# Forgetting attention: key blocks aligned with the query tiles, first 16 keys of two heads handled together

## The reference

```python
starts = [0] + list(range(N_META, L, BLOCK_Q))       # 0, 16, 144, 272, 400
ends = starts[1:] + [L]
for q0, q1 in zip(starts, ends):
    tpos = jnp.arange(q0, q1)[:, None]
    spos = jnp.arange(q1)[None, :]
    causal = spos <= tpos
    ...
    s = jnp.einsum('bhqd,bhkd->bhqk', qb[:, :, q0:q1], kb[:, :, :q1]).astype(jnp.float32) * scale
    s = s + c[:, :, q0:q1, None] - c[:, :, None, :q1]
    p = jax.nn.softmax(jnp.where(causal, s, -jnp.inf), axis=-1)
    out_fox.append(jnp.einsum('bhqk,bhkd->bhqd', p.astype(vb.dtype), vb[:, :, :q1]))
```

## Time and profile before

| | us |
|---|---|
| median of 3 runs | 1782.82 |
| lowest and highest of them | 1781.14, 1783.95 |
| the profiled execution's own time | 1780.38 |
| its span, from first to last instruction | 1778.4 |
| attention steps in it (500 to 636) | 136 |
| one pair of heads in the loop | 30.2 |

### The profile page before, as it was taken

How to read it: one execution, slowest core, us unless ns; L and a number is a source line. 1 busy time by engine, 2 the same in 40 slices (tenths; PEclk the granted TensorE clock), 3 DMA queues, 4 the chain that set the end, 5 groups by cost and what they waited for, 6 DMA issues and landing times.

```text
span 1778.4 us, 34436 instructions
## 1 busy us (share of the span) xinstructions
PE 1756.8 (99%) x13692; PEld 1702.2 (96%) x13692; DVE 1403.8 (79%) x2020; ACT 942.1 (53%) x1554; POOL 65.1 (4%) x170
## 2 busy tenths in 40 slices
PE   8999999999999999999999999999999999999998
PEld 8999999999988899999999999999999988899997
DVE  7857998779978857947998789479987688499975
ACT  5534655565567744533655545336555445266555
POOL 0000000002122201000000000000000000000000
PEclk9999999999999999999999999999999999999999
DMA  5242333336564422333333333333333323244332
GB/s 165 75 131 84 109 106 96 99 87 195 175 173 133 119 60 84 95 107 84 109 107 96 100 91 96 108 83 109 106 96 88 91 71 107 71 119 119 96 93 74
DMA packets 335157, 187.07 MB, mean 105 GB/s; under 512 B 18976, under 2 KB 325728, under 8 KB 335008
## 3 DMA queue, kind: packets, MB, share of 16 engines
q1 hardware_dynamic: 331568, 175.63, 35.3%
q0 software_dynamic: 2608, 8.72, 1.3%
q10 hardware_dynamic: 832, 0.62, 0.1%
HBM read 171.51 MB, written 10.82 MB: 103 GB/s over the span
## 4 chain that ended last, share of the span: by engine, by line
PE 82%; DVE 10%; issue 3%; ACT 3%; DMA 1%; SPq 0%; POOL 0%; DVEq 0%; ACTq 0%; POOLq 0%
PE pair L2577 46%; PE pair L2549 17%; PE pair L2518 8%; PE pair L2911 3%; PE pair L2564 1%; PE pair L847 1%; DVE w_lo L1995 1%; PE pair L2753 1%; DVE w_lo L2011 1%; PE pair L2840 1%; DVE w_lo L2006 1%; PE pair L2786 1%; PE pair L831 1%; DVE sums_w L1979 1%; PE pair L788 1%
## 5 line engine op out<-in xcount | busy, mean ns | idle before, releaser
L2577 PE MATMUL pair<-b_hi,w_hi 128*128 128x264 f32 (+1 forms) x1464 | 416.7, 285 | 2.0 <-DVE b_lo L2146 1.6
L2577 PE MATMUL pair<-b_hi,w_lo 128*128 128x264 f32 (+1 forms) x1464 | 414.7, 283 | 0.0
L2577 PE MATMUL pair<-b_lo,w_hi 128*128 128x264 f32 (+1 forms) x1464 | 414.6, 283 | 0.0
L2577 PEld LDWEIGHTS pair<-b_hi,w_hi 128*128 128x128 f32 x1464 | 275.8, 188 | 4.2 <-issue 2.9
L2577 PEld LDWEIGHTS pair<-b_lo,w_hi 128*128 128x128 f32 x1464 | 275.9, 188 | 0.0
L2577 PEld LDWEIGHTS pair<-b_hi,w_lo 128*128 128x128 f32 x1464 | 275.5, 188 | 0.0
L1513 ACT ACTIVATE w_hi<-sums_w 128x1024 fp32r<-128x1024 f32 x188 | 198.6, 1056 | 104.1 <-PE pair L2577 61.0
L1513 ACT ACTIVATE w_hi<-raw_all 128x1024 fp32r<-128x1024 f32 (+1 forms) x188 | 158.9, 845 | 141.7 <-PE pair L2577 100.1
L2577 PE MATMUL pair<-blocks_hi,w_hi 128*128 128x264 f32 (+1 forms) x816 | 231.7, 284 | 0.8 <-ACT parts L1696 0.8
L2577 PE MATMUL pair<-blocks_hi,w_lo 128*128 128x264 f32 (+1 forms) x816 | 231.2, 283 | 0.0
L2577 PE MATMUL pair<-blocks_lo,w_hi 128*128 128x264 f32 (+1 forms) x816 | 231.2, 283 | 0.0
(11 more groups left out here) (344 smaller groups left out, 3809.9 us busy)
## 6 DMA issues: line engine op xcount, KB each, us to landing
raw_all<-in_w_ffn_in SPq DMA_DIRECT2D x173, 512.0 KB, 3.9
raw_all<-in_w_ffn_out SPq DMA_DIRECT2D x64, 512.0 KB, 4.3
raw_all<-in_w_ffn_out SPq DMA_DIRECT2D x32, 384.0 KB, 3.6
raw_all<-in_w_attn_in SPq DMA_DIRECT2D x24, 512.0 KB, 4.4
qk_dram<-qk_hi POOLq DMA_DIRECT2D x16, 264.0 KB, 4.1
qk_dram<-qk_lo POOLq DMA_DIRECT2D x16, 264.0 KB, 2.9
raw_all<-in_w_attn_out SPq DMA_DIRECT2D x8, 512.0 KB, 4.8
head_v<-v_tok SPq DMA_DIRECT2D x16, 160.0 KB, 2.6
```

The source lines that it names most:

```text
L2577: mm = nc.tensor.matmul(dst, w[slot][:, c0 + kk * P:c0 + (kk + 1) * P], rhs(v, kk), start=(fresh and kk == 0 and w is w_hi and v == 0), st ...
```

## The change

**Blocks.** A forgetting tile's own key blocks now start at key 16, so they are aligned with the query tiles: s + 1 blocks of 128 keys, and the first 16 keys apart. The values of kind 1 are laid out alike (`value_tile`): four tiles from key 16 on, and keys 0 to 15 as the fifth.

**The first 16 keys.** The first head's probabilities start at column 0 of `probs[s]`, the second head's at column 16. Since both heads of a pair use the same buffer for the same s, the first head's 16 first-key columns stay at 0 to 15 and the second head's land at 16 to 31. `turn` of the second head transposes these 32 columns (with what stands behind them, 128 in all) in one block. `fox_values` of the second head multiplies 32 partitions: 16 keys of one head and 16 of the other, against a fifth tile of `head_v[1]` whose partitions 0 to 15 hold the first head's values in their 64 columns, and whose partitions 16 to 31 hold the second's.

**The small tile** is turned and multiplied once a pair, at g = 4, with both heads' 16 columns, instead of at g = 0 and g = 4.

**Staging and zeroing.** `stage_v` takes four tiles of kind 1, and for the second head two more small copies. The copies of kind 1 in pair 0 wait for a third zeroing on GpSimd. The memsets of padding columns go, and so do ScalarE's waits on them.

```diff
-        first_probs = sb("first_probs", [P, META], F32, late)
-        first_turned = sb("first_turned", [P, META], F32, late)
+        first_probs = sb("first_probs", [P, 2 * META], F32, late)
+        first_turned = sb("first_turned", [2 * META, META], F32, late)
...
-        def probs_pad(s):
-            return probs[s][:, META + (s + 1) * P:(s + 2) * P]
+        def own_probs(g):
+            at = META * (g // 4)
+            return probs[g % 4][:, at:at + fox_tile(g)[1]]
+        def own_block(g, b):
+            at = META * (g // 4) + META + b * P
+            return probs[g % 4][:, at:at + P]
+        def meta_probs(g):
+            return probs[g % 4][:, 0:P]
...
+        def value_tile(kind, jt):
+            if kind == 0:
+                return key_tile(jt)
+            return (META + jt * P, P) if jt < QT - 1 else (0, META)
...
             def stage_v(hp, e, kinds=(0, 1)):
                 for kind in kinds:
-                    sp.dma_start(head_v[e][:, kind, :, HD * e:HD * (e + 1)],
-                                 v_tok[:, kind, :, bass.ds((2 * hp + e) * HD, HD)]).then_inc(staged_v[e], 16)
+                    tiles = slice(0, QT - kind)
+                    sp.dma_start(head_v[e][:, kind, tiles, HD * e:HD * (e + 1)],
+                                 v_tok[:, kind, tiles, bass.ds((2 * hp + e) * HD, HD)]).then_inc(staged_v[e], 16)
+                if e == 1 and 1 in kinds:
+                    for a in range(2):
+                        sp.dma_start(head_v[1][META * a:META * (a + 1), 1, QT - 1, HD * a:HD * (a + 1)],
+                                     v_tok[0:META, 1, QT - 1, bass.ds((2 * hp + a) * HD, HD)]).then_inc(staged_v[e], 16)
...
+                if kind == 1:
+                    sp.wait_ge(v_zero, 3)
...
                 sc = p_psum(g)
-                for b in range(s + 2):
-                    cols = slice(b * P, (b + 1) * P)
-                    mm = nc.tensor.transpose(sc[:, cols], probs[s][:, cols], ident[:, :])
-                if s == 0:
+                for b in range(s + 1):
+                    mm = nc.tensor.transpose(sc[:, b * P:(b + 1) * P], own_block(g, b), ident[:, :])
+                if e == 1:
+                    mm = nc.tensor.transpose(sc[:, (s + 1) * P:(s + 2) * P], meta_probs(g), ident[:, :])
+                if g == 4:
                     pe.wait_ge(first_p, 2 * hp + e + 1)
-                    mm = nc.tensor.transpose(sc[0:META, FIRST_T:FIRST_T + P], first_probs[:, :], ident[:, :])
+                    mm = nc.tensor.transpose(sc[0:2 * META, FIRST_T:FIRST_T + P], first_probs[:, :], ident[:, :])
...
-                for b in range(s + 2):
-                    mm = nc.tensor.matmul(o_main[:, 1, q0 - META:q0 - META + P], head_v[e][:, 1, b, :],
-                                          turned_p[s][:, b, :], start=(g == 0 and b == 0), stop=True,
-                                          skip_group_check=True)
-                if s == 0:
-                    mm = nc.tensor.matmul(o_first[:, 1, :], head_v[e][:, 1, 0, :], first_turned[:, :],
+                own = o_main[:, 1, q0 - META:q0 - META + P]
+                for b in range(s + 1):
+                    mm = nc.tensor.matmul(own, head_v[e][:, 1, b, :], turned_p[s][:, b, :],
+                                          start=(g == 0 and b == 0), stop=True, skip_group_check=True)
+                meta_v = head_v[1][0:2 * META, 1, QT - 1, :]
+                if e == 1:
+                    mm = nc.tensor.matmul(own, meta_v, turned_p[s][0:2 * META, s + 1, :],
+                                          start=False, stop=True, skip_group_check=True)
+                if g == 4:
+                    mm = nc.tensor.matmul(o_first[:, 1, :], meta_v, first_turned[:, :],
                                           start=False, stop=True, skip_group_check=True)
...
-                    act.wait_ge(first_zero, 4)
+                    act.wait_ge(qk_low_done, QK)
+                    act.wait_ge(first_zero, 1)
...
-                if first and g < 3:
-                    act.wait_ge(first_zero, 4 + g)
+                if first and g == 1:
+                    act.wait_ge(drained, ph.n0 + QKV)
...
-                if s == 0:
-                    nc.vector.tensor_copy(first_turned[0:META, :], src[0:META, FIRST_T:FIRST_T + META])
-                nc.vector.tensor_copy(turned_p[s][:, :, :],
-                                      src[:, 0:(s + 2) * P].rearrange("p (b q) -> p b q", q=P)).then_inc(pt_out, 1)
+                if g == 4:
+                    nc.vector.tensor_copy(first_turned[:, :], src[0:2 * META, FIRST_T:FIRST_T + META])
+                n = s + 1 + g // 4
+                nc.vector.tensor_copy(turned_p[s][:, 0:n, :],
+                                      src[:, 0:n * P].rearrange("p (b q) -> p b q", q=P)).then_inc(pt_out, 1)
...
-                nc.gpsimd.memset(v_tok[:, 1, QT - 1, :], 0.0).then_inc(v_pad, 1)
-                pool.wait_ge(v_pad, 2)
+                pool.wait_ge(sp_masked, 1)
...
+                        nc.gpsimd.memset(head_v[1][0:META, 1, QT - 1, HD:2 * HD], 0.0).then_inc(v_zero, 1)
+                        pool.wait_ge(v_zero, 3)
```

More of the change, by code:

```diff
@@ L453, in fox_tile, with own_first @@
             return META + (g % 4) * P, 2 * META + P - META + (g % 4) * P
-        def probs_pad(s):
-            return probs[s][:, META + (s + 1) * P:(s + 2) * P]
+        def own_probs(g):
[6 more added lines that the diff above has]
+            return probs[g % 4][:, 0:P]
+        def own_first(g):
+            at = META * (g // 4)
+            return first_probs[0:META, at:at + META]
         def p_psum(g):
@@ L629, in v_turned_out @@
             kind, jt = r // QT, r % QT
-            _, kn = key_tile(jt)
+            _, kn = value_tile(kind, jt)
             eng.wait_ge(vt_turned, r + 1)
-            if jt == QT - 1:
-                eng.wait_ge(v_pad, kind + 1)
+            if r == QT - 1:
+                eng.wait_ge(v_pad, 1)
             copy(v_tok[0:kn, kind, jt, :], v_bank(r)[0:kn, :]).then_inc(vt_odd if r % 2 else vt_even, 1)
@@ L726, in turn_v @@
                 kind, jt = r // QT, r % QT
-                t0, kn = key_tile(jt)
+                t0, kn = value_tile(kind, jt)
                 if r == 0 or r == QT:
@@ L823, in stick_values @@
                 if s == 0:
-                    pe.wait_ge(staged_v[e], 32 * hp + 32)
+                    pe.wait_ge(staged_v[e], 32 * (e + 1) * (hp + 1))
                     if isinstance(hp, int) and hp == 0:
@@ L977, in act_probs @@
                 count_ge(act, p_turned, c - 1)
-                nc.scalar.activation(probs[s][:, 0:nk], s_psum(g)[:, 0:nk], ACT.Exp, scale=-1.0,
+                nc.scalar.activation(own_probs(g), s_psum(g)[:, 0:nk], ACT.Exp, scale=-1.0,
                                      bias=stats[:, g % 2, 0:1], accum_out=stats[:, g % 2, 1:2]).then_inc(p_exp, 1)
                 if s == 0:
-                    nc.scalar.activation(first_probs[0:META, :], s_psum(g)[0:META, FIRST_S:FIRST_S + META], ACT.Exp,
+                    nc.scalar.activation(own_first(g), s_psum(g)[0:META, FIRST_S:FIRST_S + META], ACT.Exp,
                                          scale=-1.0, bias=stats[0:META, 2, 0:1],
@@ L1303, in dve_probs @@
                 dve.wait_ge(p_inv, c + 1)
-                p = probs[s][:, 0:nk]
+                p = own_probs(g)
                 nc.vector.tensor_scalar(p, p, stats[:, g % 2, 2:3], None, ALU.mult).then_inc(p_done, 1)
@@ L1309, in dve_probs @@
                     dve.wait_ge(first_inv, 2 * hp + e + 1)
-                    nc.vector.tensor_scalar(first_probs[0:META, :], first_probs[0:META, :], stats[0:META, 2, 2:3], None,
+                    nc.vector.tensor_scalar(own_first(g), own_first(g), stats[0:META, 2, 2:3], None,
                                             ALU.mult).then_inc(first_p, 1)
@@ L3039, in _ @@
                 pool.wait_ge(first_zero, 1)
-                nc.gpsimd.memset(first_turned[:, :], 0.0).then_inc(first_zero, 1)
-                for i, s in enumerate((0, 3)):
-                    pool.wait_ge(first_zero, 2 + i)
-                    nc.gpsimd.memset(probs_pad(s), 0.0).then_inc(first_zero, 1)
                 pool.wait_ge(c_low, 2)
@@ L3072, in _ @@
                 pool.wait_ge(p5_done, ph.pairs[-1].s + 1)
-                nc.gpsimd.memset(v_tok[:, 1, QT - 1, :], 0.0).then_inc(v_pad, 1)
-                pool.wait_ge(v_pad, 2)
+                pool.wait_ge(sp_masked, 1)
                 ones_and_pad(1)
-                pool.wait_ge(drained, ph.n0 + QKV)
-                for i in range(2):
-                    pool.wait_ge(first_zero, 4 + i)
-                    nc.gpsimd.memset(probs_pad(1 + i), 0.0).then_inc(first_zero, 1)
-                pool.wait_ge(first_zero, 6)
                 def pool_step_(hp, g, first):
```

## The result

| | before | after |
|---|---|---|
| median of 10 runs | 1781.39 | 1784.55 |
| lowest and highest | 1780.33, 1783.95 | 1783.21, 1789.42 |
| profiled execution's span | 1778.4 | 1782.0 |
| its mean granted clock | 0.999 | 0.997 |

The changed kernel takes 3.2 us more: a ratio of 1.0019, with a 95% interval from 1.0010 to 1.0027. That is inside the predicted range and just inside the 0.2% called "same" (the interval reaches beyond it), but the sum had said +0.6. The missing 2.6 us turned out to be something the sum had no term for.

What follows compares the result with a forecast made beforehand. TensorE, busy for 99% of the span, was taken as the bound. Pair 0 at -0.83, three loop pairs at +0.09 each and the drain at +1.14 gave +0.6 us: 1783.4, range 1778.4 to 1786.4.

Steps and rivals of the forecast that it cites:

- pair 0: First pair of heads: fewer transposes and shorter copies, later savings and one 32-partition multiplication hidden; -0.83 us.
- the sum: All terms added over the pairs and the final drain: 15 d - 5.12, +0.6 us at d = 0.38.
- The work removed: First head's transposes, value blocks and small tile: 1.57 us of TensorE a pair, 1.24 of it on the path.
- ScalarE's split of g = 2: Late next in a pair's early part: cuts the saving there from 0.47 to 0.36 us, so 1.13 a pair.
- steps 4 to 7: Pair after `sticks` of g = 3 starts: removed transpose and value blocks, 0.33 and 0.44 us, all on the path.
- The detour: Second head's `fox_values`, g = 4 to 7: each 32-partition multiplication among 128-partition ones costs TensorE d = 0.38 us; 16 in all.
- Rival B: 32 partitions behave like 68, with no gap (d = 0): -4.2 us, 1778.6; chance 0.15.
- rival C: Gap also inside the pair of float32 instructions (d = 0.65): +4.6 us, 1787.4; chance 0.11.
- The detours of steps 7, 1 and 2: 32-partition multiplications of g = 4, 6 and 7: 0.38 us each, all on the path except 0.19 at g = 4.
- the slack: At g = 4's 32-partition multiplication: VectorE is ready 0.19 us before the low part, so 0.19 is hidden.
- A pair in the loop: Each pair after the first changes by 4 d - 1.43, +0.09 us with d = 0.38.
- step 3: One transpose and 0.36 us of `fox_values` of g = 0 go; hidden, as `sticks` of g = 3 waits for VectorE.

Runs made afterwards that it cites:

- Full rows with fill: Changed kernel with the first keys' and small tile's multiplications on 128 partitions, plus four extra multiplications a pair at TensorE's two waits: 1777.20 us, ratio 0.9970.
- before_16: Kernel before, with the last block in the second head's `fox_values` multiplied on 16 partitions instead of 128: 1787.30 us, ratio 1.0024.
- the two kernels with fill: Changed kernel plus four unread multiplications a pair at TensorE's two waits, 1782.06 us; the same with 128 partitions in place of 32, 1777.20 us.
- before_fill: Kernel before plus four extra, unread multiplications a pair at the same two places: 1783.40 us, ratio 1.0004.
- full rows: Changed kernel with the first keys' and small tile's multiplications on all 128 partitions, extra rows zeroed, no extra multiplications: 1782.39 us, ratio 0.9993.

## Why the prediction came out as it did

**The work removed: right.** The prediction gave 1.24 us a pair on the path, and 1.13 with ScalarE's split of g = 2 as what is late next. Full rows with fill show 1.24, with the split's share in it, so 0.11 more than the 1.13. In parts: from the pair's start to `sticks` of g = 3 it was 12.94 (572.08 to 585.02 in the earlier trace rows) and is 12.59 (570.20 to 582.79), 0.35 less where 0.36 was forecast, so the split does take its 0.11; from there to the next pair's start it is 0.90 less (17.26 and 16.36) where 0.77 was forecast. That extra 0.13 in steps 4 to 7 I did not trace further. In pair 0 the start of `sticks` at 539.12 has moved to 538.62, 0.9 earlier once the later start of attention (0.4) is taken off, where 0.8 was forecast.

**The detour: right in kind, a little large.** d = 0.38 was taken from the pooling mixer; 0.34 was measured in the chain, in `before_16` and between the two kernels with fill. Rival B (d = 0) and rival C (d = 0.65) are both out. The choice of the nearest rows, the 16-partition ones and not the 68-partition ones, carried this.

**The detours of steps 7, 1 and 2: partly hidden, by more than the sum had.** For step 7 the prediction put 0.38 - 0.19 = 0.19 on the path. Its reading of the slack holds where nothing else was changed. This is VectorE's timeline in `before_16`, where the softplus work ends at 600.32:

```profile
600.32 0.57 DVE L1285 TENSOR_TENSOR v_rows<-v_rows,b_rows 128x400 f32<-128x400 f32 x1
601.29 0.69 DVE L1321 COPY c_room<-pair 128x512 f32<-128x512 f32 x1 [0.41 <-PE pair L810]
601.90 0.68 DVE L1299 TENSOR_TENSOR qk_lo<-v_rows,qk_hi 128x512 fp32r<-128x512 f32 x1
```

The low part comes 1.58 after that end, against 1.40 in the earlier trace rows (597.39 to 598.79, the former from the same timeline), and the copy 0.97 after it, against 0.59: of 0.38, 0.20 is hidden. VectorE's timeline after:

```profile
598.70 0.69 DVE L1355 COPY c_room<-pair 128x512 f32<-128x512 f32 x1 [0.26 <-PE pair L839]
599.30 0.68 DVE L1332 TENSOR_TENSOR qk_lo<-v_rows,qk_hi 128x512 fp32r<-128x512 f32 x1
```

Here the low part comes only 1.43 after the end of the softplus work at 597.87, and 1.40 in the full rows with fill. Two things make the difference. The detour is shorter in this step, as TensorE's timeline shows:

```profile
597.14 0.38 PE L877 MATMUL pair<-c_room,head_v 128*128 128x128 f32 x2
597.46 0.48 PE L881 MATMUL pair<-c_room,head_v 32*128 32x128 f32 x2
597.78 0.29 PE L884 MATMUL pair<-first_turned,head_v 32*128 32x16 f32 x2
598.00 0.55 PE L837 MATMUL pair<-ident,sq 128*128 128x128 f32 x3
```

From the last full block to the transposes it is 0.86, where 0.22 + 0.22 + 0.14 = 0.58 would do: 0.28. And work was removed ahead of it, so TensorE reaches this place 0.06 earlier against VectorE's row (with full rows and fill the transposes start 0.14 ahead of the end of the softplus work, before 0.08 ahead). Of the 0.28, 0.25 is hidden and 0.03 is left.

Of the detours of g = 6 and 7, 0.13 is hidden: the copy of g = 1 comes 0.68 later after the pair's start than in the full rows with fill (7.08 against 6.40), the low part ahead of `sticks` of g = 3 only 0.55 later (12.39 against 11.84). In between lies ScalarE's split of g = 2. In `before_16` the same two detours count in full (13.61 from the pair's start to `sticks` of g = 3, against 12.94), so what hides them here is probably the 0.11 that this split takes back as long as nothing delays TensorE. A pair in the loop is then -1.24 + 0.34 + 0.03 + 0.68 - 0.13 = -0.32; measured at full clock, 29.87 - 30.20 = -0.33. The forecast was +0.09.

**The clock: left out.** This is the step of the sum that failed: a term is missing. The prediction wrote of step 3 that the work taken out there "is hidden, because `sticks` of g = 3 waits for VectorE afterwards, and this wait only grows", and priced a growing wait at nothing; the waits that grew are the two of step 4. The granted clock was in front of the reader all along, as 1.00 in the earlier trace rows and 0.999 for the span, and was read as a constant. What the runs showed in its place: each fall costs 1.67 us, five times what a detour does, and filling the two waits of step 4 takes it away. Of the span's +3.6, the edits account for -0.5, the clock for +3.3, and 0.8 lies outside attention. The time fell into the range, but not for the reasons in the sum: its +0.6 had no clock in it, and its detours were too dear by 0.4 us a pair. That the range held is in part luck: two errors of opposite sign, and a width meant for the price of the detour.

The Trainium skill, page TensorE: Matmul & The Clock Gate, section Why this matters for your kernels, names idle gaps of TensorE between bursts of multiplications as what sends the clock back to half. The trace agrees in kind, since waits stand ahead of each fall; but these are 0.34 and 0.42 us inside a dense row of work, which a reader of that rule would not call gaps between bursts.

**What stays open.** The traces show two waits, about 2 us apart, at or just ahead of each fall in attention, most often 0.34 and then 0.41 or 0.42 us long; the profiles with these two filled have no fall there, except the one behind other waits in `before_fill`, and filling elsewhere doesn't prevent it. They don't show why it comes in pairs 1 and 3 of the profiled execution and not in pair 2, whose waits are the same (0.34 and 0.42), nor why it differs from run to run. The runs of before at 0.997 are taken to have such falls too, but none of them has a trace. Making ScalarE and VectorE earlier in step 4, which would end the waits with no added work, was not tried.

## What to carry to other kernels

Before pricing removed work at nothing because "the wait behind it only grows", look at the granted clock in that stretch; a short row of waits on an engine that is otherwise full can cost more than the work was worth, and the loss shows up as busy time. Compare kernels at equal mean clock first, and then their clocks by stretch, since the mean also counts the idle end: sorted so, the 3.2 us here turned out to be the clock's. Where an operand of 16 or 32 partitions stands among full ones, bring it to full height with zeros (68 partitions showed no such cost): with that and one spare multiplication at each of the two waits, this change gives 1776.99 us, 0.31% below the kernel before (0.9969, 0.9958 to 0.9980), instead of 0.19% above it.

## What the runs showed of the hardware

In the 5 us ahead of a fall of the changed kernel TensorE is busy for 4.25. One pair later the same work has the same 4.25, and nothing falls; nor does it in the kernel before, with 4.22 between pairs 0 and 1 (the rows are after, after, before):

```profile
550.00:555.00 5.00, 4.25 (x29) 3.55 (x29) 4.60 (x12) 4.25 (x10) 0.74 (x2) 1.00 0.50 114
581.50:586.50 5.00, 4.25 (x30) 3.56 (x28) 4.60 (x12) 4.27 (x10) 0.74 (x2) 1.00 0.50 116
534.70:539.70 5.00, 4.22 (x28) 3.33 (x27) 4.73 (x10) 4.15 (x10) 0.74 (x2) 1.00 0.66 169
```

So such a stretch can be followed by a fall and need not be. Work that nobody needs can be a gain: 2 instructions, 0.22 us, at each of two places of a pair take 5 us off the kernel with full rows. And a multiplication of 16 or 32 partitions of 128 columns costs about 0.34 us more than one of 128, for the same result.
